# The column groups of the small gates added up by two fp32r matmuls instead of one plain fp32 matmul

## The reference

```
p = xn @ w_in[l]
(aq, ak, av, ao, ai, af, bb, bc, bx, cz, cxbc, cdt,
 sq, sk, sv, gates) = jnp.split(p, SPLIT_POINTS, axis=-1)
ya = mlstm(aq, ak, av, ao, ai + a_igate_b[l], af + a_fgate_b[l], a_norm_g[l])
...
yc = mamba2_mixer(cz, cxbc, cdt, ...)
```

## Time and profile before

| | |
|---|---|
| median of three runs | 991.52 us |
| time of the profiled execution | 991.83 us |
| its span | 990.3 us |
| TensorE matmul busy | 982.1 us |
| VectorE busy | 669.0 us |
| ScalarE busy | 467.6 us |
| mean granted clock of TensorE | 0.999 |

### The profile page before, as it was taken

How to read it: one execution, slowest core, us unless ns; L and a number is a source line. 1 busy time by engine, 2 the same in 40 slices (tenths; PEclk the granted TensorE clock), 3 DMA queues, 4 the chain that set the end, 5 groups by cost and what they waited for, 6 DMA issues and landing times.

```text
span 990.3 us, 12156 instructions
## 1 busy us (share of the span) xinstructions
PE 982.1 (99%) x4376; PEld 798.8 (81%) x4376; DVE 669.0 (68%) x897; ACT 467.6 (47%) x585; POOL 52.2 (5%) x72
## 2 busy tenths in 40 slices
PE   9999999999999999999999999999999999999997
PEld 7887788778777887777888888888888888888886
DVE  6885776777686676555363547677777777764765
ACT  7575466545548233444432333544444444432646
POOL 0720000000000000000000000000000000001200
PEclk9999999999999999999999999999999999999999
DMA  7575222143322333342242322383323232367942
GB/s 250 198 146 156 79 71 67 64 117 107 98 88 81 121 140 135 110 142 97 85 182 95 105 88 87 105 171 106 106 85 106 88 103 85 106 255 189 202 76 86
DMA packets 49867, 118.22 MB, mean 119 GB/s; under 512 B 20373, under 2 KB 21525, under 8 KB 49697
## 3 DMA queue, kind: packets, MB, share of 16 engines
q1 hardware_dynamic: 26784, 90.57, 27.1%
q0 software_dynamic: 6160, 24.70, 10.7%
q10 hardware_dynamic: 16880, 2.37, 1.5%
HBM read 113.38 MB, written 4.25 MB: 119 GB/s over the span
## 4 chain that ended last, share of the span: by engine, by line
PE 96%; ACT 1%; DVE 1%; issue 1%; DMA 1%; SPq 0%; ACTq 0%
PE gb L537 72%; PE xb L874 5%; PE xb L600 3%; PE xb L537 2%; PE gb L874 2%; PE gb L854 2%; PE xb L854 2%; PE xb L810 1%; PE gb L721 1%; PE xb L707 1%; PE xb L768 1%; DMA raw<-w_stream 1%; PE gb L919 1%; PE gb L648 1%; PE gb L600 1%
## 5 line engine op out<-in xcount | busy, mean ns | idle before, releaser
L1415 DVE TENSOR_TENSOR w_lo<-raw,w_hi 128x1024 fp32r<-128x1024 f32 x144 | 178.4, 1239 | 181.0 <-ACT w_hi L950 180.5
L950 ACT ACTIVATE w_hi<-raw 128x1024 fp32r<-128x1024 f32 x145 | 153.3, 1058 | 274.8 <-PE gb L537 266.1
L537 PE MATMUL gb<-xn_hi,w_hi 128*128 128x512 f32 x720 | 282.2, 392 | 0.0
L537 PE MATMUL gb<-xn_hi,w_lo 128*128 128x512 f32 x720 | 280.3, 389 | 0.0
L537 PE MATMUL gb<-xn_lo,w_hi 128*128 128x512 f32 x720 | 280.2, 389 | 0.0
L537 PEld LDWEIGHTS gb<-xn_hi,w_hi 128*128 128x128 f32 x720 | 135.2, 188 | 28.5 <-issue 0.8
L537 PEld LDWEIGHTS gb<-xn_hi,w_lo 128*128 128x128 f32 x720 | 135.1, 188 | 28.3
L537 PEld LDWEIGHTS gb<-xn_lo,w_hi 128*128 128x128 f32 x720 | 135.2, 188 | 27.8 <-issue 0.2
L537 PE MATMUL gb<-y_hi,w_hi 128*128 128x512 f32 x352 | 138.4, 393 | 0.0
L537 PE MATMUL gb<-y_hi,w_lo 128*128 128x512 f32 x352 | 137.0, 389 | 0.0
L537 PE MATMUL gb<-y_lo,w_hi 128*128 128x512 f32 x352 | 137.0, 389 | 0.0
(11 more groups left out here) (340 smaller groups left out, 1279.1 us busy)
## 6 DMA issues: line engine op xcount, KB each, us to landing
raw<-w_stream SPq DMA_DIRECT2D x147, 512.0 KB, 3.3
wr<-w_quad POOLq DMA_DIRECT2D x16, 512.0 KB, 8.1
abc<-scr_a POOLq DMA_DIRECT2D x8, 640.0 KB, 4.2
wv<-v_quad POOLq DMA_DIRECT2D x8, 512.0 KB, 5.5
wr<-w_quad SPq DMA_DIRECT2D x8, 512.0 KB, 5.9
x_in<-xT SPq DMA_DIRECT2D x8, 256.0 KB, 5.7
wv<-v_quad SPq DMA_DIRECT2D x4, 512.0 KB, 5.0
x<-xT POOLq DMA_DIRECT2D x1, 2048.0 KB, 8.6
```

The source lines that it names most:

```text
L537: ins = pe.matmul(out, w[:, r, lo:hi], rhs(k)[x], start=(first and n == 0 and q == 0), stop=(last_ and n == len(ks) - 1 and q == 2))
L950: act.activation(w_hi[:, r, 0:n], raw[:, r, 0:n], ACT.Copy).then_inc(S["hi_ready"], 1)
L1415: dve.tensor_tensor(w_lo[:, r, 0:n], raw[:, r, 0:n], w_hi[:, r, 0:n].bitcast(F32), ALU.subtract)\
```

## The change

The copy of the summed columns is split into a high part (ScalarE) and a low part (VectorE), both fp32r, and the selection matrix is copied to fp32r. Two fp32r matmuls, added into the same bank, take the place of the plain one. The buffer `sel_r` lies where `colT` is written later, `g_hi` and `g_lo` behind `g_in`. TensorE waits for one more semaphore ahead of the two matmuls. The new block of ScalarE stands in its step for u = 22 behind the block with Abs, Exp and Ln; that of VectorE behind the masking of the scores.

```diff
--- before.py
+++ after.py
@@ -161,6 +161,7 @@
     tri_r = m.put("tri_r", [P, P], F32R)
     ones_r = m.put("ones_r", [P, P], F32R)
     causal = m.put("causal", [P, P])
+    sel_r = at("sel_r", [P, 96], F32R, m.at)
     colT = m.put("colT", [P, NB, P])
     vec = m.put("vec", [P, N_VEC])
     fcw = vec[:, V_FCW:N_VEC].rearrange("p (t c) -> p t c", c=4)
@@ -226,6 +227,7 @@
     later_lo = at("later_lo", [P, 6 * P], F32R, C0 + 12 * 4 * T)
     later_hi = at("later_hi", [P, 5 * P], F32R, C0 + 2 * 4 * T)
     g_in = g.put("g_in", [P, T])
+    g_hi, g_lo = (g.put(n, [P, T], F32R) for n in ("g_hi", "g_lo"))
     assert g.at <= C0 + 12 * 4 * T
 
     g = Map(A0)
@@ -687,7 +689,9 @@
 
                 pe.wait_ge(S["g_sel"], 1)
                 pe.wait_ge(S["psum_read_dve"], order[first_tile[U_SMALL]][1])
-                pe.matmul(GB[3][0:96, :], sel[:], g_in[:], start=True, stop=True).then_inc(S["g_sum"], 1)
+                pe.wait_ge(S["xg_ready"], KD + 1)
+                pe.matmul(GB[3][0:96, :], sel_r[:], g_hi[:], start=True, stop=False)
+                pe.matmul(GB[3][0:96, :], sel_r[:], g_lo[:], start=False, stop=True).then_inc(S["g_sum"], 1)
 
             if u == U_SMALL + 10:
                 pe.wait_ge(S["g_rows"], 1)
@@ -1138,6 +1142,11 @@
                 act.wait_ge(S["d_soft"], 2 * h + 2)
                 act.activation(later_hi[:], later[:, 0:5 * P], ACT.Copy).then_inc(S["d_sp_hi"], 1)
 
+            if u == U_SMALL:
+                act.wait_ge(S["g_sel"], 1)
+                act.activation(sel_r[:], sel[:], ACT.Copy)
+                act.wait_ge(S["psum_read_dve"], order[first_tile[U_SMALL]][1])
+                act.activation(g_hi[:], g_in[:], ACT.Copy).then_inc(S["xg_hi"], 1)
             if s == U_SMALL + 3:
                 table(EXP_LN)
                 act.wait_ge(S["g_split"], 1)
@@ -1659,6 +1668,9 @@
                 split_lo(sp_lo[:], t1[:], sp_hi[:]).then_inc(S["d_sp_lo"], 1)
                 dve.wait_ge(S["d_sp_hi"], 2 * h + 2)
                 split_lo(later_lo[:, 0:5 * P], later[:, 0:5 * P], later_hi[:]).then_inc(S["d_sp_lo"], 1)
+            if u == U_SMALL:
+                dve.wait_ge(S["xg_hi"], KD + 1)
+                split_lo(g_lo[:], g_in[:], g_hi[:]).then_inc(S["xg_ready"], 1)
             if s - 5 in D_AT:
                 h = D_AT.index(s - 5)
                 dve.wait_ge(S["d_hi"], h + 1)
```

## The result

The changed kernel takes 994.38 us (median of ten executions, 993.13 to 995.3), the kernel before 991.65 (ten, 991.35 to 991.97): a ratio of 1.0027 with a 95% interval of 1.0019 to 1.0035. It is slower by 2.7 us, the forecast was 993.6. What the medians hide is the spread: 2.2 us where the kernel before has 0.6.

A forecast was written before the change was run, and what follows sets the result against it. TensorE's matmul stream was taken to bound the kernel. Pause 2.38 us, plus 0.10 exposed weight load, less 0.40 saved makes +2.08; on 991.52 that forecasts 993.6 us, range 992.8 to 994.4.

The forecast's parts named there:

- What bounds the kernel: Whole kernel: TensorE's matmuls fill 99% of the span; a microsecond added at 100 us comes out nearly whole.
- The matmuls: TensorE between units 23 and 24: plain fp32 matmul 0.86 us, two flowing fp32r matmuls 0.46, saving 0.40.
- The chain of the inputs: Copies behind Ln on ScalarE, then VectorE: TensorE stands still from 99.77 to 102.15, 2.38 us.
- Moved behind it: ScalarE's and VectorE's later splits come 0.70 us later, covered by TensorE's own 2.08 us delay, costing nothing.
- The clock falls in the new gap: Rival, chance 0.03: TensorE's mid-kernel pause of 2.4 us lowers the clock, 1 to 3 us on top, 994.6 to 996.6.
- the reading of the end of the span: Last matmuls end by 984.4, clock still full from 984, 0.50 from 989; so a 2.4 us pause should leave it alone.
- The warning that I cited: Trainium skill, cited for the clock rival: idle gaps between mid-kernel bursts of matmuls bring the clock back to half.
- its line at 0.2%, 2.0 us: Whole-kernel limit of what a measurement can tell from no change; slower by over 0.2% was given 0.53.

The follow-up runs named there:

- the early inputs: Changed kernel with ScalarE's new block ahead of Abs, Exp and Ln instead of behind them: 990.76 us.
- the lower group: Changed kernel, first ten executions plus eight repeated without edit: the eight faster executions, without the upper group's lower clock, mean 993.3 us.
- the late sum: Changed kernel with TensorE's two matmuls behind unit 24 instead of behind unit 23, copies left in place: 990.58 us.
- the two kernels without a pause: Changed kernel with ScalarE's copies ahead of Abs, Exp and Ln (990.76 us), or with TensorE's two matmuls behind unit 24 (990.58 us).
- the copies alone: Changed kernel with all copies kept but made for nothing; TensorE uses the plain fp32 matmul without waiting for them: 991.28 us.
- the filler: Changed kernel with ten thrown-away fp32r matmuls of 512 columns put ahead of TensorE's wait: 993.28 us.
- the shorter pause: Changed kernel with ScalarE's new block between Exp and Ln, TensorE idle for 1.06 us: 992.06 us.
- the longer pause: Changed kernel with two more 128x512 copies, made for nothing, ahead of `g_hi`; TensorE's pause 3.35 us: 995.6 us.
- the plain sum: Changed kernel with TensorE's wait for `g_lo` kept, but the sum done by one plain fp32 matmul: 995.0 us.

## Why the prediction was right, and where it was not

*What bounds the kernel*: right. No other wait took the 2 us in, and busy time from 110 to 970 is the same to 0.01 us.

*The matmuls*: right. Due time to unit 24: 0.86 for the plain one, 0.46 for the pair without a pause (99.02 to 99.48 with the early inputs).

*The chain of the inputs*: right, but for two links that nearly cancel.

| | predicted | measured |
|---|---|---|
| `sel_r` start to `g_hi` start | 0.16 | 0.17 |
| `g_hi` | 0.62 | 0.61 |
| hand-over, `g_lo` | 0.04, 0.69 | 0.04, 0.69 |
| hand-over to TensorE | 0.06 | 0.15 |
| pause (due time to the pair's start) | 2.38 | 2.47 |
| pair to unit 24 | 0.56 | 0.51 |
| sum | +2.08 | +2.12 |

Of these two the hand-over to TensorE is 0.09 longer, the restart of the pair 0.05 shorter (the second of the pair starts 0.28 behind the first, not 0.33): from `g_lo`'s end (101.58) to unit 24 (102.24) it is 0.66 in place of 0.62. The estimate for the 96-column copy from the Trainium skill ("ScalarE: Activation LUTs", "What ACT_TABLE_LOAD costs": 186 ns and 0.833 ns an element, 93 ns of overlap, so 0.17 to the next start) is met by the row: 0.27 us long, 0.17 to `g_hi`.

*Moved behind it*: right; the sum behind unit 24 runs with these splits as late, and without a loss.

*The clock falls in the new gap*: here the prediction failed. It gave this rival 0.03, and it happens in about half of the executions. It is what lifts the median to +2.7: the lower group alone is at +1.7 to +1.8. The step that failed was the reading of the end of the span: there the clock was still full 3.6 us after the last matmul, and I took this for what a pause of 2.4 us may count on. One row was one draw. The same place in two other profiles, the changed kernel and the late sum:

```profile
990.00:991.00 1.00, 0.00 (x0) 0.00 (x0) 0.00 (x0) 0.00 (x0) 0.00 (x0) 1.00 0.52 171
991.00:992.00 1.00, 0.00 (x0) 0.00 (x0) 0.00 (x0) 0.00 (x0) 0.00 (x0) 0.51 0.00 0
```

```profile
985.00:986.00 1.00, 0.00 (x0) 0.00 (x0) 0.88 (x2) 0.91 (x2) 0.00 (x0) 0.63 0.00 0
```

In the changed kernel the last matmul ends at 985.9 and the clock is full up to 991, five microseconds on; with the late sum it ends at 983.4 and the clock falls within the window from 985, two microseconds on. In all ten profiles of this case the fall comes 1.9 to 5.1 us after TensorE's last matmul; the row that I read, with 4.6, was among the later ones. The three falls in mid-kernel come 2.6, 3.3 and 4.5 us after TensorE stopped, in the same range, though it had been at work again for 0.3 to 1.2 us by then. So a row that shows a late fall promises nothing for a pause of 2.3 us: the fall can come 1.9 us after TensorE stops, and it can come when the pause is already over. How the draw is made no run shows. The warning that I cited, from the Trainium skill's "TensorE: Matmul & The Clock Gate", section "Why this matters for your kernels", names only gaps longer than this one; here 2.3 us were enough in nine of eighteen executions, and the measurement decides. The price I gave, 1 to 3 us, holds: it is 1.6 by the profile and 1.7 between the groups.

So the terms of the sum were right in the main, but that the outcome fell on the forecast's side was luck. The forecast had its line at 0.2%, 2.0 us. The wait alone, as the lower group has it, is +1.7 to +1.8 us, 0.18%, and lies below that line; the median is over it only by the case that I had all but ruled out. And 994.38 lies 0.02 us inside the range's upper end of 994.4, a range that left that case out. It is also a median between two groups, a time that few executions have.

*Open*: the lower group's mean of 993.3 is 0.4 under the sum (991.6 + 2.1), and the two kernels without a pause are 0.4 and 0.6 under theirs; the copies alone, the filler and the shorter pause lie 0.2, 0.4 and 0.3 under theirs. The profiles have 0.27 us of this, in a place where the forecast had put nothing. Behind the last matmul VectorE adds up and ScalarE squares; first the kernel before, then the changed one:

```profile
984.40 0.42 DVE L2044 TENSOR_TENSOR x<-x,gb 128x256 f32<-128x256 f32 x1 [2.46 <-PE gb L919]
985.19 0.42 ACT L1384 ACTIVATE f_sq<-x 128x256 f32<-128x256 f32 x1 [2.38 <-DVE x L2044]
```

```profile
985.98 0.42 DVE L2056 TENSOR_TENSOR x<-x,gb 128x256 f32<-128x256 f32 x1 [2.46 <-PE gb L923]
986.50 0.42 ACT L1393 ACTIVATE f_sq<-x 128x256 f32<-128x256 f32 x1 [2.10 <-DVE x L2056]
```

ScalarE starts 0.37 us behind VectorE's end before, 0.10 with the change, and 0.10 in the profiles of all eight experiments too, that of the copies alone among them. Why it starts later in the kernel before, of which there is one profile, no run shows. The rest of the shortfalls, 0 to 0.3 us (0.4 with the longer pause), no experiment here told apart.

## What to carry to other kernels

A cheaper instruction on the engine that bounds is only worth its saving (0.40 us here) if its new inputs are ready at its place in that engine's order; find the place where the producer's queue puts them, not where its idle time would. Here either of two moves, of the copies or of the sum, turns 994.4 us into 990.8 or 990.6. When TensorE is made to pause, count the pause and, with a chance of its own, the clock behind it (here none of eleven at 1.1 us, about half at 2.3, five of five at 3.3), and look at the spread of the executions and their mean clock before trusting a median.

## What the runs showed of the hardware that was not expected

The granted clock can fall after a pause is over, and in all three profiles of a fall in mid-kernel it did. TensorE started again at 101.48, 102.08 and 102.63 us (the plain sum, the changed kernel, the longer pause), and the clock fell at 101.8, 103.1 and 103.8. It does not come back at once when the work is dense again: in the changed kernel the windows from 103 to 107 have 0.54, 0.50, 0.50 and 0.76, with TensorE busy in all of them. The low stretch is 3.4 us long in each of the three, so one fall costs the same, 1.6 us, whether the pause ahead of it was 2.3 or 3.3 us: what differed with the pause was how often it came, not what it cost.
